# Two-block transformer kernel: window sums of the compressed keys on GpSimd, and a new spread of the top-k selection rounds

## The reference, cut to what matters

```
k_blocks = k_br[:, :, 0][:, tok] + nsa_cmp_pe[0][:, None, :]
k_c = jnp.einsum('bnlgd,lde->bnge', k_blocks, w_nsa_cmp[0])
```

## Time and profile before

| | us |
|---|---|
| three runs | 2520.18, 2523.76, 2527.74 (median 2523.76) |
| profiled execution | 2526.07 |
| its span | 2523.9 |
| PE busy in it | 2429.9 (96%) |
| DVE busy | 1228.2 (49%) |
| POOL busy | 1227.3 (49%) |
| ACT busy | 930.3 (37%) |
| PE's mean granted clock | 0.98 of full |

### The profile page before, as it was taken

The page is one execution under the profiler, slowest core; times in us unless marked ns, Lnnn a source line. Parts: engine busy times, 40 slices in busy tenths (PEclk is TensorE's granted clock), DMA queues, the critical chain, the costliest instruction groups (busy, mean ns, idle before and its releaser), DMA issues.

```text
span 2523.9 us, 33202 instructions
## 1 busy us (share of the span) xinstructions
PE 2429.9 (96%) x12413; PEld 1945.3 (77%) x12413; DVE 1228.2 (49%) x2251; ACT 930.3 (37%) x1471; POOL 1227.3 (49%) x1594
## 2 busy tenths in 40 slices
PE   7899999999999999999999999998998998999999
PEld 5778777888888778877788878887665667788887
DVE  6885653452335668356333143255688644511211
ACT  5233442432322532244242232244335755423322
POOL 3444445555556645354555555565333432555554
PEclk9999999999999999999999999999898899999999
DMA  4222322332222232222233223233210011222222
GB/s 158 85 81 72 92 67 91 107 105 99 94 98 92 92 101 79 82 84 72 88 100 125 95 90 100 88 105 109 75 63 18 2 38 39 99 93 100 94 99 92
DMA packets 81294, 218.57 MB, mean 87 GB/s; under 512 B 15856, under 2 KB 25456, under 8 KB 80752
## 3 DMA queue, kind: packets, MB, share of 16 engines
q1 hardware_dynamic: 61920, 200.96, 24.3%
q10 hardware_dynamic: 19216, 15.51, 2.2%
HBM read 207.78 MB, written 2.10 MB: 83 GB/s over the span
## 4 chain that ended last, share of the span: by engine, by line
PE 83%; DVE 11%; ACT 2%; issue 2%; ACTq 1%; POOL 1%; DMA 0%; DVEq 0%
PE psG L1007 25%; PE psG L1009 24%; PE psG L1008 24%; PE psT L1184 2%; PE psS L1163 2%; DVE work_b L2048 1%; PE psO L1217 1%; DVE work_m L2048 1%; DVE tmp L2048 1%; ACTq L1700 1%; DVE work_b L2513 1%; PE psS L1094 1%; DVE max L2512 1%; DVE small_work L2048 1%; PE psG L1163 0%
## 5 line engine op out<-in xcount | busy, mean ns | idle before, releaser
L946 POOL TENSOR_TENSOR w_lo<-w_raw,w_hi 128x256 fp32r<-128x256 f32 (+1 forms) x1482 | 1156.2, 810 | 1188.4 <-ACT w_hi L1569 1188.3
L1007 PE MATMUL psG<-h_hi,w_hi 128*128 128x512 f32 x1880 | 751.1, 400 | 12.4 <-POOL w_lo L946 4.1
L1008 PE MATMUL psG<-h_lo,w_hi 128*128 128x512 f32 x1880 | 737.1, 392 | 0.0
L1009 PE MATMUL psG<-h_hi,w_lo 128*128 128x512 f32 x1880 | 736.8, 392 | 0.0
L1569 ACT ACTIVATE w_hi<-w_raw 128x1024 fp32r<-128x1024 f32 (+4 forms) x417 | 404.0, 969 | 501.1 <-PE psG L1009 485.8
L1007 PEld LDWEIGHTS psG<-h_hi,w_hi 128*128 128x128 f32 x1880 | 356.3, 189 | 103.7 <-issue 18.4
L1009 PEld LDWEIGHTS psG<-h_hi,w_lo 128*128 128x128 f32 x1880 | 355.7, 189 | 75.4
L1008 PEld LDWEIGHTS psG<-h_lo,w_hi 128*128 128x128 f32 x1880 | 356.7, 190 | 73.0 <-issue 1.9
L1007 PE MATMUL psG<-m_hi,w_hi 128*128 128x512 f32 x800 | 311.8, 390 | 1.1 <-DVE m_lo L2048 1.1
L1009 PE MATMUL psG<-m_hi,w_lo 128*128 128x512 f32 x800 | 311.5, 389 | 0.0
L1008 PE MATMUL psG<-m_lo,w_hi 128*128 128x512 f32 x800 | 311.4, 389 | 0.0
(11 more groups left out here) (359 smaller groups left out, 2592.5 us busy)
## 6 DMA issues: line engine op xcount, KB each, us to landing
w_raw<-wstream SPq DMA_DIRECT2D x327, 512.0 KB, 3.3
w_raw<-wstream SPq DMA_DIRECT2D x64, 256.0 KB, 2.6
w_raw<-wstream SPq DMA_DIRECT2D x16, 384.0 KB, 3.0
work_b<-work_b ACTq DMA_DIRECT2D x16, 256.0 KB, 3.8
work_b<-cmpw ACTq DMA_DIRECT2D x2, 2048.0 KB, 8.9
x<-xT SPq DMA_DIRECT2D x4, 512.0 KB, 7.9
small_work<-ssmp ACTq DMA_DIRECT2D x8, 256.0 KB, 2.8
outT<-x SPq DMA_DIRECT2D x8, 256.0 KB, 2.0
```

Of the source, the lines that this page charges most:

```text
L946: ins = pool.tensor_tensor(lo[:, c], w[:, c], hi[:, c].bitcast(F32), ALU.subtract)
L1007: pe.matmul(out, whi, hi, start=(k == 0), stop=False)
L1008: pe.matmul(out, whi, lo, start=False, stop=False)
L1009: ins = pe.matmul(out, wlo, hi, start=False, stop=(k == K - 1))
```

## The change

Four edits.

1. The window additions of `kc` and `vc` leave DVE. POOL does them, between two weight tiles: after the split of the third tile behind `kc` (or `vc`), before the fourth.
2. The number of rounds in a slot is looked up by its product, and is zero from `uq3` on.
3. PE multiplies the identity five times (256 columns each) before it waits for the last outputs of the projections. The result is not used.
4. ACT computes the exponent of one value at the head of the attention.

```
-SELECT_EACH = 3
+SELECT_EACH = {("p2", "kc"): 2, ("kvd",): 1, ("p2", "vs"): 3, ("kd",): 1, ("p2", "vw"): 3, ("uq", 0): 1, ("p2", "qn0"): 3,
+               ("uq", 1): 1, ("p2", "vc"): 2, ("p2", "qn1"): 3, ("uq", 2): 1, ("p2", "qn2"): 2}
...
-            each = SELECT_EACH if s_ < len(PROJECTIONS) else 1 if steps[chosen][1] == 8 else 0
+            each = SELECT_EACH.get(PROJECTIONS[s_], 0) if s_ < len(PROJECTIONS) else 0
...
+            def windows(p):
+
+                i = 0 if p["kind"] == "cmpk" else 1
+                pool.wait_ge(s_p["raw"], p["raw"])
+                if i:
+                    pool.wait_ge(s_p["cmpo"], i)
+                for l0 in (0, CMP_STRIDE):
+                    src = raws[p["i"] % 4][:, l0:l0 + CMP_STRIDE * CMP_N].rearrange("p (n l) -> p l n", l=CMP_STRIDE)
+                    pe_ = par("pe", CMP_L * i + l0, CMP_STRIDE).unsqueeze(2).to_broadcast([P, CMP_STRIDE, CMP_N])
+                    ins = pool.tensor_tensor(cmpin[:, l0:l0 + CMP_STRIDE], src, pe_, ALU.add)
+                ins.then_inc(s_p["cmpin"], 1)
+
+            windows_before = {tile_of["p2", name] + SPLIT_SLOTS + 1: by_key["p2", name] for name in ("kc", "vc")}
             for n in range(len(weights)):
                 if n in norm_before:
                     norm_low_parts(norm_before[n])
+                if n in windows_before:
+                    windows(windows_before[n])
...
             project(block2_posts)
+            who, count = taken[[key for key in PROJECTIONS if number[key] % GEMM_BANKS == 2][-1]]
+            pe.wait_ge(s_took[who], count)
+            for i in range(5):
+                pe.matmul(psG[:, 2, 0:2 * P], ident, CON[:, 0:2 * P], start=True, stop=True)
             pe.wait_ge(s_p["out"], block2_done["out"])
...
             def attention(us, side=None):
                 la = ahead(us[0])
+                do(act.activation(stat[:, 3, 11:12], eps, ACT.Exp))
...
-            def windows(p):
-
-                i = 0 if p["kind"] == "cmpk" else 1
-                dve.wait_ge(s_p["raw"], p["raw"])
...
-                    if new and new["kind"] in ("cmpk", "cmpv"):
-                        windows(new)
```

## The result

The changed kernel takes 2529.69 us (median of 22 runs, 2523.22 to 2532.3), the kernel before 2526.3 in the same runs (22, 2520.18 to 2529.09). The ratio is 1.0014, interval 1.0008 to 1.0019: some 3.5 us slower. I had forecast 5.3 us less (2518.5, against the 2523.76 of that time), and the range ended at 2527. Direction and range are both missed.

What follows compares the result with a forecast made beforehand. DVE was taken to pace the projections: 2526.07 - 12.7 (attention starts earlier) + 7.4 (attention longer) = 2520.8 us for the profiled execution, so 2518.5 for the median, 2.3 lower; range 2505 to 2527.

Steps and rivals of the forecast that it cites:

- What bounds the kernel, the rounds' places: Projections before the attention: DVE paces them; 19 of 42 rounds move from there into the attention.
- DVE's load, 26.1 us less: Projections: moved rounds with their mask addition and threshold pass take 21.9 us off DVE, windows 4.2.
- The first contraction at 1807.6: Projections: PE starts its first contraction at 1807.6 instead of 1808.72, because the relu before it comes early.
- I get 1862.9 for it: PE waits 3.1 us there: Second contraction: starts at 1862.9 after a new 3.1 us wait for a relu; the lead falls to 6.8 us.
- `qn3` ends at 1889.5: 7.7 us ahead: Last projections: `uq3` and `qn3` follow without DVE's rounds, so `qn3` ends 7.7 us earlier than before.
- the third rival: Second contraction: larger wait, windows last; projections give 7.5 us, attention takes 7.4, total 2523.7; chance 0.13.
- "8.6 us" from `qn3` to the attention: End of projections: ACT's 2.9 us and two DVE queries of 2.8 each make 8.6 us, instead of 13.5.
- the term of 12.7 us for the attention's start: Projections as a whole: the attention starts at 1898.1 instead of 1910.76, 12.7 us won; bounds 5 and 26.
- Windows on POOL, 3.8 us a pair: Projections: POOL takes 1.9 us per window addition, 3.8 a pair, between 2.5 and 6.7, hidden behind other work.
- The multiplications and the exponent, 1.6 us at the head: Head of the attention: full clock for the first scores and shorter score waits save 1.6 us; ends 0 and 3.
- The attention, +7.4: Attention: returning rounds cost 9.0 us, less 1.6 at the head, so 7.4 longer; bounds 1.7 and 20.3.
- What follows the attention is unchanged: After the attention: a run of full products, taking the same time as before.

Runs made afterwards that it cites:

- A: Changed kernel with the window additions back on DVE, all else kept: ratio 0.9997 to the kernel before, median 2526.05 us.
- F: Kernel before with only the new number of rounds per slot: ratio 1.0006, median 2527.12 us.
- D: Changed kernel without ACT's early exponent: ratio 1.0015 to the kernel before, median 2529.07 us.
- K: Kernel before with windows on POOL and three rounds a slot, but none in the last two projections: ratio 0.9989, median 2522.22 us.
- C: Changed kernel without PE's five multiplications by the identity: ratio 1.0013 to the kernel before, median 2528.95 us.
- M: Changed kernel with block 2's 17 rounds in the slots up to `uq0`, without multiplications and exponent: ratio 0.9987 to the kernel before, median 2521.91 us.
- L: Changed kernel with the same 23 rounds, block 2's 17 of them in the slots up to `uq0`: ratio 0.9986 to the kernel before, median 2521.34 us.
- J: Changed kernel with one round moved from `vc`'s slot to `qn1`'s and windows back on DVE: ratio 0.9995 to the kernel before, median 2523.61 us.

## Why the prediction was wrong, step by step

- *What bounds the kernel, the rounds' places: right.* Windows, waits and the planner's count held. *DVE's load, 26.1 us less: 20.6 measured.* What left is as counted; the passes that stayed grew, as told above.
- *The first contraction at 1807.6: wrong by 3 us.* It came at 1810.57. I let DVE's relief through and never asked what POOL's windows would do to a DVE pass beside them; one took 1.78 instead of 0.69, PE waited 1.83 for the reciprocal behind it, and then ran at half clock. Against A and F (19.7) the pass is 1.1 us of the delay and the clock the other 1.6; the second part is missing in D and K, so it does not come every time. The contraction made up for this: it lasted 3.92 us instead of 5.29, so that `vw` and `vc` ended within 0.9 us of the forecast.
- *"I get 1862.9 for it: PE waits 3.1 us there": right in kind, low in size.* It began at 1865.38 and waited 3.66. Of the 2.5 us between, 1.8 are three DVE passes ahead of the weighting that run beside POOL: 1.48, 1.02 and 0.97 in the fence above, where the kernel before has 0.38, 0.69 and 0.56 for the same. A fourth, at 1852.72, took 1.09 instead of 0.69, beside a weight split; DVE was never idle between it and the weighting. The new wait was known before the run and underpriced: I charged 3.1 us and the one-slot edit gives back 6.4 at the scores.
- *"`qn3` ends at 1889.5: 7.7 us ahead": the step that failed.* It ended at 1896.75. Of a lead of 4.4 at the second contraction, 1.9 went to its half clock (6.88 against 4.93) and 2.0 to the stretch up to `qn2`'s product, 4.8 us instead of 2.8, where the extra pair stands at the low clock. Between the products of `qn2` and `qn3` it is 7.1 us, as in the kernel before: I had let these slots go faster once the rounds had left, but DVE is idle there for ACT, which has `qn2`'s take, a rounding and four copies ahead of the root (ACT's timeline, then DVE's).

```profile
1883.89 0.69 ACT L1820 ACTIVATE work_b<-psG,params 128x512 f32<-128x512 f32 x1 [5.88 <-PE psG L1025]
1884.48 0.59 ACT L1824 ACTIVATE tmp<-psG 128x512 f32<-128x512 f32 x1
1885.52 1.06 ACT L1589 ACTIVATE w_hi<-w_raw 128x1024 fp32r<-128x1024 f32 x1 [0.45 <-ACT tmp L1824]
1886.48 1.55 ACT L1861 ACTIVATE work_b<-psS,params 128x128 f32<-128x128 f32 x4
1888.06 0.27 ACT L1845 ACTIVATE small_work<-psT,params 128x8 f32<-128x8 f32 x1
```

```profile
1888.43 0.20 DVE L2604 RECIPROCAL small_work<-small_work 128x8 f32<-128x8 f32 x1 [7.91 <-ACT small_work L1845]
```

It is the third rival that came true in its heading, "the second contraction eats the lead", but not in its mechanism: the windows did not come last, and the contraction took the clock with it, which the rival did not have.
- *"8.6 us" from `qn3` to the attention: 9.9.* DVE's first query of the two took 3.9 us instead of 2.8: beside weight splits its small `TENSOR_SCALAR` pair took 1.01 and `work_m<-work_b,consts` 1.12, against 0.38 and 0.69.

In sum the term of 12.7 us for the attention's start was 4.2: 7.1 of the 8.5 missing are lost by the end of `qn3` and 1.3 behind it.

- *Windows on POOL, 3.8 us a pair: 2.5 measured,* the low end. Hidden, as forecast, at their own price; the price on DVE was not in the sum.
- *The multiplications and the exponent, 1.6 us at the head:* the scores took 1.13 instead of 2.08, and the table load left the chain, but neither the total (C, D, M) nor the attention's length (F and M against A and L) shows either. The five took 4.0 us, between the 4.9 and the 2.5.
- *The attention, +7.4: measured +7.44, and that is luck.* The 7.4 was 9.0 for the rounds less 1.6 for the head. F has the rounds alone and is 7.4 longer, so the rounds cost 7.4 and the head gave nothing: two errors of 1.6 cancel. It is not the clock either, whose mean over the attention is 0.90 in both kernels. By stretches: start to turn 6 -1.25 (forecast -0.5), turns 6 to 18 +4.2 (+3.3), 19 to 27 +2.1 (+2), 28 to 36 +3.0 (+2.6), the rest -0.6. These windows answer the last four of the earlier trace rows (the first two of those are one here):

```profile
1931.48:1973.07 41.59, 37.77 (x356) 25.54 (x356) 35.02 (x103) 30.37 (x63) 16.26 (x24) 0.96 0.01 1
1973.07:1995.25 22.18, 20.26 (x200) 14.13 (x195) 19.63 (x70) 16.41 (x43) 9.13 (x16) 0.92 0.01 2
1995.25:2014.97 19.72, 16.05 (x136) 10.71 (x134) 17.79 (x71) 12.84 (x43) 7.43 (x16) 0.76 0.01 2
```

- *What follows the attention is unchanged: 1.5 us off.* `out2`'s product began at half clock, 0.63 us a matmul instead of 0.40, in this execution and in J's and K's; the others had 0.40. PE's timelines, of before and of after:

```profile
2046.76 0.47 PE L1007 MATMUL psG<-h_hi,w_hi 128*128 128x512 f32 x1 [1.68 <-DVE h_lo L2048]
```

```profile
2050.09 0.77 PE L1023 MATMUL psG<-h_hi,w_hi 128*128 128x512 f32 x1 [1.68 <-DVE h_lo L2069]
```

Had the sum been made with 4.2 in place of 12.7, it would have been 2526.07 - 4.2 + 7.4 + 1.5 = 2530.8; the profiled execution took 2530.55.

The Trainium skill has a rule that I had not weighed. "GPSIMD Engine Reference", section Key points, says that GpSimd shares its SBUF interfaces with VectorE and contends with DVE instructions of two SBUF inputs (or in a two-port mode). The trace agrees: `work_m<-raw_tile,consts` was 1.78 us beside POOL's windows, the pass that reads PSUM (`tmp<-psS,consts`) stayed at 0.69 through the same stretch. The small `TENSOR_SCALAR` has one tensor input and grew too; whether it runs in such a mode no run here shows. The page's figures gave an estimate of 3.2 us a pair; the trace has 2.49 and 2.54, and the measurement decides.

## What to carry to other kernels

Moving work off the engine that is busiest gains only where that engine's result is the one that arrives last; ask it of each wait, and ask again after each other part of the change, since here the windows were worth +4 us with one schedule and nothing or less with the other. A schedule that releases one chain by the progress of another (pairs by rounds) has to be followed to where the released work lands: one round in another slot was worth 7 us. Rounds that fit between an engine's waits are free: look for their place by adding them back until the anchor behind moves, rather than by equal shares.

## What was not expected of the hardware

The same 128 small multiplications took 3.9 us when PE had hardly waited before them and 6.7 to 7.0 after an idle time near 4 us, 1.9 us longer than in the kernel before, where the granted clock had dropped too (0.54 from 1865 to 1872 in the changed kernel, 0.78 from 1869 to 1875 in the kernel before). Two DVE passes beside POOL's windows took 1.1 us more each (0.69 to 1.78, and 0.38 to 1.48 for two small ones), nearly the length of one of POOL's two operations, 1.25: as if DVE stood still until it was done. The small ones have one tensor each, so it is not only a matter of two tensor inputs. Nor is it a matter of the windows: the kernel before has it beside POOL's weight splits (timelines of DVE and of POOL):

```profile
1901.61 1.14 DVE L2055 TENSOR_SCALAR small_work<-small_work 128x8 f32<-128x8 f32 x2
```

```profile
1899.95 2.77 POOL L946 TENSOR_TENSOR w_lo<-w_raw,w_hi 128x256 fp32r<-128x256 f32 x4 [5.35 <-ACT w_hi L1569]
```

The same pair takes 0.38 us where POOL is idle. And the unchanged first 1780 us ended up to 6.6 us apart between profiled executions, as much as the effects studied here, so that places have to be counted from an anchor ahead of the change.
